# Latent attention: two half-array passes for two neighbouring score pieces, and seven slots of turned probabilities

## The reference, cut to what matters

```python
q = jnp.concatenate([q_nope, q_rope], axis=-1)      # 128 + 64 features, four heads
k = jnp.concatenate([k_nope, k_rope (one for all heads)], axis=-1)
scale = (MLA_NOPE + MLA_ROPE) ** -0.5
bias = jnp.where(_chunk_mask(qp, kpos), 0.0, NEG)
s = jnp.einsum('bhqd,bhkd->bhqk', qb, k) * scale + bias
p = jax.nn.softmax(s, axis=-1)
return jnp.einsum('bhqk,bhkv->bhqv', p, v)
```

## Time and profile before

| | |
|---|---|
| runs | 2601.32, 2600.6, 2601.21 us, median 2601.21 us |
| span of the profiled execution | 2600.7 us, 35372 instructions |
| its own device time | not given apart from the runs; the span lies 0.5 us under their median |
| TensorE busy, matmuls | 2540.5 us, 12220 of them |
| VectorE, ScalarE, GpSimd busy | 1614.7, 1212.5, 332.0 us |
| mean granted TensorE clock | 0.997 |
| data moved | 398.59 MB, mean 153 GB/s |

### The profile page before, as it was taken

How to read it: one execution, slowest core, us unless ns; L and a number is a source line. 1 busy time by engine, 2 the same in 40 slices (tenths; PEclk the granted TensorE clock), 3 DMA queues, 4 the chain that set the end, 5 groups by cost and what they waited for, 6 DMA issues and landing times.

```text
span 2600.7 us, 35372 instructions
## 1 busy us (share of the span) xinstructions
PE 2540.5 (98%) x12220; PEld 2114.9 (81%) x12220; DVE 1614.7 (62%) x3499; ACT 1212.5 (47%) x2183; POOL 332.0 (13%) x368
## 2 busy tenths in 40 slices
PE   8999999999999999999999999999999999999997
PEld 7998888777667999977877888888888888888886
DVE  6123306998995776654458677876757465564765
ACT  6112314777764555554544333533335353443554
POOL 1110002222221222210000000000000001111143
PEclk9999999999999999999999999999999999999999
DMA  7334458553332111135677767657655365776787
GB/s 232 122 106 125 126 163 253 143 135 87 93 131 90 36 31 45 41 110 158 194 247 220 221 200 237 218 182 216 190 161 179 110 221 108 171 167 162 203 162 137
DMA packets 329436, 398.59 MB, mean 153 GB/s; under 512 B 21408, under 2 KB 235664, under 8 KB 320944
## 3 DMA queue, kind: packets, MB, share of 16 engines
q1 hardware_dynamic: 311696, 364.41, 44.7%
q0 software_dynamic: 17568, 31.99, 8.4%
HBM read 239.86 MB, written 156.48 MB: 152 GB/s over the span
## 4 chain that ended last, share of the span: by engine, by line
PE 62%; DVE 3%; DMA 1%; ACT 1%; issue 1%; SPq 0%; POOL 0%; DVEq 0%; ACTq 0%; POOLq 0%
PE ff_ps_x L3262 26%; PE ff_ps_m L3262 13%; PE ff_ps_z L3262 6%; PE ml_ps_s L2139 6%; PE ff_ps_m L1695 4%; PE ml_ps_o L2168 4%; PE ml_ps_t L2152 2%; DMA ml_v_raw<-scr_yT 1%; DMA ff_pieces<-scr_acc 0%; PE ff_ps_r L2699 0%; PE mo_ps_t L2716 0%; SPq L2326 0%; DVE ff_pieces L2429 0%; DVE ff_pieces L2620 0%; DVE ff_pieces L2616 0%
## 5 line engine op out<-in xcount | busy, mean ns | idle before, releaser
L3262 PE MATMUL ff_ps_x<-ff_mv_hi_p,ff_st_hi_p 128*128 128x512 f32 x764 | 297.8, 390 | 0.5 <-ACT ff_u L3002 0.5
L3262 PE MATMUL ff_ps_x<-ff_mv_hi_p,ff_st_lo_p 128*128 128x512 f32 x764 | 297.3, 389 | 0.0
L3262 PE MATMUL ff_ps_x<-ff_mv_lo_p,ff_st_hi_p 128*128 128x512 f32 x764 | 297.2, 389 | 0.0
L2139 PE MATMUL ml_ps_s<-wide,ml_qs 128*128 128x416 f32 (+14 forms) x880 | 195.6, 356 | 3.7 <-PEq L137 2.7
L3108 DVE TENSOR_TENSOR ff_st_lo_p<-ff_ps_m,ff_st_hi_p 128x512 fp32r<-128x512 f32 x190 | 130.8, 689 | 103.4 <-ACT ff_st_hi_p L2985 103.4
L2952 POOL DMA_DIRECT2D scr_acc<-ff_pieces x64 | 55.5, 872 | 1015.3 <-DVE ff_pieces L3132 946.9
L3002 ACT ACTIVATE ff_u<-ff_ps_x 128x512 f32<-128x512 f32 x128 | 76.6, 598 | 215.0 <-PE ff_ps_x L3262 215.0
L3262 PEld LDWEIGHTS ff_ps_x<-ff_mv_hi_p,ff_st_hi_p 128*128 128x128 f32 x764 | 143.4, 188 | 32.4 <-issue 2.0
L3262 PEld LDWEIGHTS ff_ps_x<-ff_mv_hi_p,ff_st_lo_p 128*128 128x128 f32 x764 | 143.4, 188 | 29.9
L3262 PEld LDWEIGHTS ff_ps_x<-ff_mv_lo_p,ff_st_hi_p 128*128 128x128 f32 x764 | 143.4, 188 | 29.6
L2139 PEld LDWEIGHTS ml_ps_s<-wide,ml_qs 128*128 128x128 f32 x880 | 152.0, 191 | 16.3 <-issue 2.9
(11 more groups left out here) (318 smaller groups left out, 6349.7 us busy)
## 6 DMA issues: line engine op xcount, KB each, us to landing
st_raw<-in_w_ff SPq DMA_DIRECT2D x64, 512.0 KB, 6.2
scr_hid<-ff_pieces SPq DMA_DIRECT2D x128, 256.0 KB, 2.7
st_raw<-scr_hid SPq DMA_DIRECT2D x64, 512.0 KB, 5.4
ring<-in_w_ff SPq DMA_DIRECT2D x28, 1024.0 KB, 7.7
scr_t<-ring SPq DMA_DIRECT2D x24, 1024.0 KB, 5.8
ring<-scr_t SPq DMA_DIRECT2D x21, 1024.0 KB, 8.1
scr_acc<-ff_pieces POOLq DMA_DIRECT2D x64, 256.0 KB, 4.1
ring<-scr_u SPq DMA_DIRECT2D x13, 1024.0 KB, 8.4
```

What stands on the lines that cost most here:

```text
L2139: m = pe.matmul(ps_s[n % NSB][:, 0:w], q, k, start=j == 0, stop=j == len(pairs) - 1)
L3262: m = pe.matmul(bank[:, :], w[kind][:, k], a[kind][:, k], start=start and k == 0 and i == 0, stop=stop and k == KH - 1 and i == 2, skip_gr ...
```

## The change

The second rotary pass is changed for pairs of pieces. Within a row block the pieces 0 and 1, 2 and 3 are paired; a piece without a partner is made as before. The first piece of a pair gets four full passes, then waits for the bank of the second piece too, then come two matmuls over 64 partitions each: the upper one (partitions 0 to 63) takes high queries x low keys into the first piece's bank and ends it, the lower one (64 to 127) takes the same product for the second piece into the second's bank and opens it. The second piece then adds its four full passes. The product low queries x low keys, which the full pass also added, is left out for paired pieces. The lower half needs the high part of the rotary queries in partitions 64 to 127, so `qs` has a fourth part and three high copies are made in place of two. To make room the slots of turned probabilities go from eight to seven; a tile `mo_y_lo` of the mixing moves into the fourth part of `qs`.

```diff
@@ -1155,8 +1155,8 @@
         self.o_out = right(ctx, "o_out", [P, 2, 512])
         with ExitStack() as place:
             self.second = right(place, "da_second", [P, 2, L])
-        self.qs = right(ctx, "ml_qs", [P, 2, 3, 512], F32R)
-        right(da_ctx, "da_second_rest", [P, 2 * L + -2 * L % P - 6 * 512])
+        self.qs = right(ctx, "ml_qs", [P, 2, 4, 512], F32R)
+        right(da_ctx, "da_second_rest", [P, 2 * L + -2 * L % P - 8 * 512])
         self.q_hi_ready, self.q_split = mem.sem("ml_q_hi_ready"), mem.sem("ml_q_split")


@@ -1579,15 +1579,16 @@
             heads(dve, {"chunk": chunk, "scale": invert, "end": end})
             dve.wait_ge(probs_ready, NT * H)
             q_raw = f32(ahead.q[:, :, :, :])
-            lower = slice(ROPE, 2 * ROPE)
+            upper, lower = slice(0, ROPE), slice(ROPE, 2 * ROPE)
             for g in range(2):

                 dve.wait_ge(ahead.latent_q_loaded[g], 16 * 3)
-                for part in range(2):
-                    dve.tensor_copy(latent.qs[:, g, 2 * part], q_raw[:, g, part]).then_inc(latent.q_hi_ready, 1)
-                dve.wait_ge(latent.q_hi_ready, 2 * g + 2)
+                dve.tensor_copy(latent.qs[:, g, 0], q_raw[:, g, 0]).then_inc(latent.q_hi_ready, 1)
+                dve.tensor_copy(latent.qs[upper, g, 2], q_raw[upper, g, 1]).then_inc(latent.q_hi_ready, 1)
+                dve.tensor_copy(latent.qs[lower, g, 3], q_raw[lower, g, 1]).then_inc(latent.q_hi_ready, 1)
+                dve.wait_ge(latent.q_hi_ready, 3 * g + 3)
                 dve.tensor_tensor(latent.qs[:, g, 1], q_raw[:, g, 0], f32(latent.qs[:, g, 0]), ALU.subtract).then_inc(latent.q_split, 1)
-                dve.tensor_tensor(latent.qs[lower, g, 2], q_raw[lower, g, 1], f32(latent.qs[lower, g, 2]),
+                dve.tensor_tensor(latent.qs[lower, g, 2], q_raw[lower, g, 1], f32(latent.qs[lower, g, 3]),
                                   ALU.subtract).then_inc(latent.q_split, 1)

         @stage.tensor
@@ -1676,7 +1677,7 @@
         self.q_hi_ready, self.q_split = latent.q_hi_ready, latent.q_split
         self.y = self.v_raw[:, 0:2 * KD].rearrange("p (u k) t -> p u k t", u=2)
         first = self.qs[:, :, :, :].rearrange("p a b n -> p (a b n)")
-        self.y_hi, self.y_lo, self.y_hi_second = (first[:, D * i:D * i + D].rearrange("p (k t) -> p k t", k=KD) for i in range(3))
+        self.y_hi, self.y_lo, self.y_hi_second, self.y_lo_second = (first[:, D * i:D * i + D].rearrange("p (k t) -> p k t", k=KD) for i in range(4))
         self.w_hi, self.w_lo = ([wide[:, k, D * i:D * i + D] for k in range(self.W_AHEAD)] for i in range(2))
         self.y_loaded = [mem.sem(f"mo_y_loaded{u}") for u in range(2)]
         self.w_loaded = [mem.sem(f"mo_w_loaded{v}") for v in range(4)]
@@ -1723,7 +1724,7 @@
         v_lo = mem.sb("ml_v_lo", [P, NT + 1, P], F32R)
         bias = ahead.bias
         rows = [mem.sb(f"ml_rows{u}", [P, 4, RP]) for u in range(2)]
-        NPT = 8
+        NPT = 7
         NTB = 3
         pT_hi = mem.sb("ml_pT_hi", [P, NPT, 512], F32R)
         pT_lo = mem.sb("ml_pT_lo", [P, NPT, 512], F32R)
@@ -1999,8 +2000,10 @@

                 act.wait_ge(scores_ready, NCH * h + first_chunk(4 * g - 4) if g >= 2 else
                             NCH * (h - 1) + (first_chunk(4 * g + 12) if g == 0 else NCH))
-                for part in range(2):
-                    act.activation(qs[:, g % 2, 2 * part], q_raw[:, g % 2, part], ACT.Copy).then_inc(q_hi_ready, 1)
+                upper, lower = slice(0, ROPE), slice(ROPE, 2 * ROPE)
+                act.activation(qs[:, g % 2, 0], q_raw[:, g % 2, 0], ACT.Copy).then_inc(q_hi_ready, 1)
+                act.activation(qs[upper, g % 2, 2], q_raw[upper, g % 2, 1], ACT.Copy).then_inc(q_hi_ready, 1)
+                act.activation(qs[lower, g % 2, 3], q_raw[lower, g % 2, 1], ACT.Copy).then_inc(q_hi_ready, 1)

             def split_next_q(h, **at):
                 if not last_head(h):
@@ -2087,11 +2090,11 @@
             def split_q(h, g, **at):
                 if first_head(h) and g < 2:
                     return
-                dve.wait_ge(q_hi_ready, 2 * (NG * h + g) + 2)
+                dve.wait_ge(q_hi_ready, 3 * (NG * h + g) + 3)
                 dve.tensor_tensor(qs[:, g % 2, 1], q_raw[:, g % 2, 0], f32(qs[:, g % 2, 0]), ALU.subtract).then_inc(q_split, 1)

                 lower = slice(ROPE, 2 * ROPE)
-                dve.tensor_tensor(qs[lower, g % 2, 2], q_raw[lower, g % 2, 1], f32(qs[lower, g % 2, 2]), ALU.subtract).then_inc(q_split, 1)
+                dve.tensor_tensor(qs[lower, g % 2, 2], q_raw[lower, g % 2, 1], f32(qs[lower, g % 2, 3]), ALU.subtract).then_inc(q_split, 1)

             def split_next_q(h, **at):
                 if not last_head(h):
@@ -2133,10 +2136,24 @@
                 cols = slice(P * b, P * b + P)
                 q_hi, q_lo, q_rope = (qs[:, g % 2, j, cols] for j in range(3))
                 k_hi, k_lo = (keys[:, j, k0:k0 + w] for j in range(2))
-                pairs = [(q_hi, k_hi), (q_hi, k_lo), (q_lo, k_hi)]
-                pairs += [(q_rope, rope_keys[:, j, k0:k0 + w]) for j in range(2)]
+                pairs = [(q_hi, k_hi), (q_hi, k_lo), (q_lo, k_hi), (q_rope, rope_keys[:, 0, k0:k0 + w])]
+                nth = n - first_chunk(i)
+                second_of_two, first_of_two = nth % 2 == 1, nth % 2 == 0 and n + 1 < NCH and chunks[n + 1][0] == i
+                if not (first_of_two or second_of_two):
+                    pairs.append((q_rope, rope_keys[:, 1, k0:k0 + w]))
                 for j, (q, k) in enumerate(pairs):
-                    m = pe.matmul(ps_s[n % NSB][:, 0:w], q, k, start=j == 0, stop=j == len(pairs) - 1)
+                    m = pe.matmul(ps_s[n % NSB][:, 0:w], q, k, start=j == 0 and not second_of_two,
+                                  stop=j == len(pairs) - 1 and not first_of_two)
+                if first_of_two:
+                    if not (first_head(h) and n + 1 < NSB):
+
+                        pe.wait_ge(scores_read, NCH * h + n - NSB + 2)
+                    k1, w1 = chunks[n + 1][1:]
+                    upper, lower = slice(0, ROPE), slice(ROPE, 2 * ROPE)
+                    m = pe.matmul(ps_s[n % NSB][:, 0:w], qs[upper, g % 2, 2, cols], rope_keys[upper, 1, k0:k0 + w],
+                                  start=False, stop=True)
+                    pe.matmul(ps_s[(n + 1) % NSB][:, 0:w1], qs[lower, g % 2, 3, cols], rope_keys[lower, 1, k1:k1 + w1],
+                              start=True, stop=False)
                 m.then_inc(scores_ready, 1)

             def turn(h, g, t, u, **at):
@@ -2383,7 +2400,7 @@
         ones = mix.v_raw[:, 2 * KD]
         g_post = mix.o_out[:, :, :].rearrange("p a n -> p (a n)")
         y = mix.y
-        y_hi, y_lo = [mix.y_hi, mix.y_hi_second], [mix.y_lo, mem.sb("mo_y_lo", [P, KD, P], F32R)[:, :, :]]
+        y_hi, y_lo = [mix.y_hi, mix.y_hi_second], [mix.y_lo, mix.y_lo_second]
         sq = y_rstd = early.pieces[:, 3 * D:3 * D + DA_H * P]
         h = early.pieces[:, 0:2 * D].rearrange("p (u n) -> p u n", u=2)
         eps = mem.sb("mo_eps", [P, 1])
```

## The result

The changed kernel takes 2611.79 us (median of five runs, 2610.86 to 2614.11) against 2601.32 us for the kernel before on the same chip. The ratio is 1.0042 with a 95% interval of 1.0029 to 1.0054: slower by 10.9 us, somewhere between 7.5 and 14. That has the sign of the forecast and lies in its range, at two thirds of the +16.6 us that the sum gave. The profiled execution took 2613.7 us with a span of 2611.9, 11.2 us over the span before.

What follows compares the result with a forecast made beforehand. TensorE was taken as the bound; per pair -0.18 + 0.06 + 0.35 = +0.23 us, over 72 pairs +16.6 us, other terms 0, giving 2617.8 us. Own range 2608 to 2626; 8 in 10: 2591 to 2627.

Steps and rivals of the forecast that it cites:

- Removed pass: Latent-attention scores on TensorE: two overlapping halves replace two full passes, saving 0.18 us per pair, 13.0 us over 72 pairs.
- Switch: TensorE going from the full array to 64 rows and back: 0.35 us per pair, bounds 0.10 and 0.55.
- Offset between the halves: The second half pass starts later because of its own weight load: 0.06 us per pair, between 0 and 0.11.
- Third copy of q: ScalarE's extra high copy per quarter, at most 8.7 us of its time, claimed hidden by idle time: 0.
- Moved wait: TensorE waits for the second piece's bank one pass earlier: at most some tenths of a us, taken as 0.
- seven slots: ScalarE's copies of turned probabilities wait for product n - 7 instead of n - 8: 0, no gain.
- gapless: Rival: half passes join TensorE's stream without a gap, -8.6 us, 2592.6 us; chance 0.26.
- no overlap: Rival: a gap, and halves streaming one after the other, +0.35 per pair, +25.2 us, 2626.4; chance 0.10.
- no effect: Rival: halves run as ordinary passes without gap, or switch and offset just cancel the gain, 2601 to 2604; chance 0.12.

Runs made afterwards that it cites:

- two entries: Changed kernel with the lower half pass moved behind the second piece's first pass, so the 64-row part is entered and left twice per pair; 2656.64 us, ratio 1.0207.
- changed, without half passes: Changed kernel with every piece given its five full passes again, the copies of q, qs parts and slots kept as changed; 2602.64 us, ratio 1.0009.
- no fifth pass: Changed kernel with four full passes and no half pass for paired pieces, the wait for the second bank kept; 2582.75 us, ratio 0.9928.

## Why the prediction was right, and where it was off

**The bound and the mechanism** hold. TensorE sets the stage, the loads around the half passes do not run under the streams beside them, and that outweighs the saved pass. Three kernels show the switch from three sides: a full pass in place of the halves (19 us faster), a second entry (0.34 to 0.37 us each), a pass on part of the columns (no gap).

**Removed pass, -0.18 per pair.** Its step is right, its worth on this path is not. Passes taken out alone brought 9 to 10 of 13.0 us and 20.1 of 27; TensorE then waited more for VectorE. I had written that "what TensorE no longer has to do in this stage comes off the time". It does to about three quarters. I had read the waits of TensorE's matmuls alone, 2.6 us; its loads wait too, 3.0 us for the low parts of turned probabilities in front of turns (the row stands with the third copy above).

**Switch, +0.35 per pair, taken from 16-row transposes.** Measured 0.37 by the parts in the timeline, 0.35 against the pass on 64 columns, 0.34 to 0.37 by the two entries. That 64 rows behave as 16 was a guess that held; nothing in the trace of before spoke for it, so that it held is in part luck. TensorEngine Tiling (Array Packing) of the Trainium skill ("Key Properties") has the drain at a change of mode, and the traces agree for rows, with 0.10 us from a stream's end to the next load in either direction. The page counts 128 rows by 64 columns as a mode too, and there the passes of the experiment follow each other at 0.20 us with no drain, so for columns the measurement decides; whether a pass with 64 active columns is run as that mode, no trace says. That the loads behind the drain lie open, half of the price, is seen only in the rows.

**Offset between the halves, +0.06 per pair.** This term was mis-sized. Both loads and both streams start together, 3 to 4 ns apart in all 72 pairs: 0.003, so 4.1 us of the 16.6 were not there. TensorE: Matmul & The Clock Gate of the Trainium skill ("Measured speedup vs the span model") has about 4 ns, which the trace confirms; I had weighed a row of loads on the same rows higher, and the experiment with both halves on the same partitions shows why that was the wrong row: there loads do step by 0.11.

**Third copy of q, 0.** Mis-sized the other way: 3.6 us (1 to 6) alone. I priced it by ScalarE's idle share in a window. The row that bore on it was VectorE's wait for these copies, which the trace of before has ten times, 3.9 us in all.

**Moved wait, 0, and seven slots, 0.** Both are confirmed by their own experiments, to within some 2 us.

**The sum.** In the timeline a pair takes 0.77 us from its last full pass to where the next is on its way, 0.57 before: +0.20, 72 times 14.4 us. At 416 columns it is 0.283 to the halves, 0.385 to the next and 0.06 to 0.10 for its open load, 0.73 to 0.77 where 0.79 was forecast. The runs gave 10.9 (7.5 to 14), the stages 14.6, and 12.7 less the clock.

What lies between is settled by one more count in the traces. TensorE's loads also stand idle at places that have nothing to do with the halves, over 0.15 us at a time, mostly for VectorE's low parts and GpSimd's rows. Added up over the stage, load by load, without the gaps in front of and right behind a half pass, and taken off together with the clock, it leaves what the passes themselves take:

| kernel | stage, us | clock | idle elsewhere | left | against before |
|---|---|---|---|---|---|
| before | 346.7 | 1.5 | 9.5 | 335.7 | |
| changed, without half passes | 349.5 | 1.5 | 12.8 | 335.2 | -0.5 |
| changed | 361.3 | 3.4 | 8.5 | 349.4 | +13.7 |
| one full pass for the halves | 339.1 | 0 | 16.4 | 322.7 | -13.0 |
| no fifth pass | 329.4 | 1.5 | 20.1 | 307.8 | -27.9 |
| two entries | 407.5 | 13.7 | 6.0 | 387.8 | +52.1 |

The last column is close to what the steps say: 14.4 us for the change, -13.0 for 72 passes, -27 for 144. The changed kernel against the one with a full pass gives 26.7 us, 0.37 for each of 72 switches, and two entries 0.36 for each of 144. So the 0.37 of the timeline is right, and on this path it costs 0.26 to 0.28 because 8 us of waits, 16.4 down to 8.5, disappear under the gaps. A removed pass loses a quarter of its worth to the same waits, and the third copy of q, 3.3 us of them without half passes, no longer shows in the changed kernel.

So the forecast of 16.6 was nearer to the steps than to the time: the offset was 4.1 us too large, and the waits elsewhere and the clock were not in the sum. Its range had a slip too: the inner half of the distance to the upper bound of 0.55 ends at 0.45 and not at 0.47, which makes 2625 of 2626 and changes nothing here.

Of the rivals, "gapless" is excluded by every timeline, "no overlap" by the kernel with both halves on one side, "no effect" by the interval.

What was not tried: several pairs' halves in one entry. By the numbers here an entry costs 0.37 us of steps and a pair saves 0.18, so as an estimate it takes three pairs in an entry to gain. That needs the banks of six pieces open at once, and there are four.

## What to carry to other kernels

Two half-height passes do share the array fully, but going in and out of it costs some 0.37 us of TensorE at 2.4 GHz, about two streams of 430 columns. By that estimate it pays only where three or more pairs of such width run in one entry; no run here shows a case that pays. Price a copy added to an idle engine by who waits for it in its place, not by the engine's idle share. An idle time that is equally long at all places of its kind is suspect of being the machine's, whatever releaser the profile names: edit the wait away and see whether the time stays. And before two traces are compared, look at the granted clock where the stage begins: here it moved stages by up to 13.7 us.

## What the runs showed of the hardware that I had not expected

Loads of the two halves start together, 3 ns apart, when they go to different rows, and 0.11 us apart when they go to the same. A single half pass pays the whole switch (2611.73 us against 2611.79 with both). The switch hangs on rows in every case tried: 128 rows by 64 columns is entered and left in the ordinary step of 0.20 us. The kernel with two entries had a mean granted clock of 0.72 in the first 50 us of the stage in its profiled execution, and its two executions with a mean clock of 0.991 and 0.992 took 10 us more than those at 0.996 and 0.997.
